# A chunked delta-rule scan in a two-layer decoder: the inverse's products on four quarters of TensorE, and the group norm inside the scan

## The reference, cut to what matters

```python
def step(state, inp):                      # for each of 16 heads of 64
    r_t, d_t, k_t, v_t, kk_t, a_t = inp
    sa = jnp.einsum('bhvk,bhk->bhv', state, -kk_t)
    state = (state * d_t[:, :, None, :] + sa[..., None] * (kk_t * a_t)[:, :, None, :]
             + v_t[..., None] * k_t[:, :, None, :])
    return state, jnp.einsum('bhvk,bhk->bhv', state, r_t)
_, y = lax.scan(step, s0, ...)
mean = jnp.mean(y, axis=-1, keepdims=True)
var = jnp.mean(jnp.square(y - mean), axis=-1, keepdims=True)
y = ((y - mean) * lax.rsqrt(var + GN_EPS)).reshape(B, S, D) * ln_g + ln_b
bonus = jnp.sum(rf * kf * r_k, axis=-1, keepdims=True) * vf
out = (y + bonus.reshape(B, S, D)) * g
return out @ w_o
```

## Time and profile before

| what | us |
|---|---|
| median of three runs | 974.61 (974.09, 974.61, 981.54) |
| profiled execution | 980.12 |
| span of its instructions | 978.3 |
| busy in it: TensorE, weight loads | 856.2, 733.1 |
| busy: VectorE, ScalarE, GpSimd | 660.2, 418.4, 112.1 |
| mean granted clock | 0.945 |

### The profile page before, as it was taken

How to read it: one execution, slowest core, us unless ns; L and a number is a source line. 1 busy time by engine, 2 the same in 40 slices (tenths; PEclk the granted TensorE clock), 3 DMA queues, 4 the chain that set the end, 5 groups by cost and what they waited for, 6 DMA issues and landing times.

```text
span 978.3 us, 17529 instructions
## 1 busy us (share of the span) xinstructions
PE 856.2 (88%) x7477; PEld 733.1 (75%) x7477; DVE 660.2 (67%) x710; ACT 418.4 (43%) x585; POOL 112.1 (11%) x175
## 2 busy tenths in 40 slices
PE   1599997678888888999999999997777899999997
PEld 1597886567776455999999878995445689999976
DVE  4897965557557375999999957365675468545553
ACT  3279222333433146444343355514664653344441
POOL 8400002232331030000000003200000000000000
PEclk9799899799999689999999999996898999999999
DMA  8922335232205307799999556742000538655551
GB/s 322 338 89 85 100 116 197 76 118 88 89 13 189 129 20 258 259 372 368 368 370 384 201 172 208 213 140 77 1 1 1 173 129 278 238 175 194 192 172 43
DMA packets 71837, 170.16 MB, mean 174 GB/s; under 512 B 5432, under 2 KB 6736, under 8 KB 71760
## 3 DMA queue, kind: packets, MB, share of 16 engines
q1 hardware_dynamic: 68784, 160.75, 47.0%
q0 software_dynamic: 2416, 7.15, 2.5%
q10 hardware_dynamic: 560, 1.14, 0.3%
HBM read 166.42 MB, written 1.05 MB: 171 GB/s over the span
## 4 chain that ended last, share of the span: by engine, by line
PE 52%; DVE 34%; ACT 7%; issue 3%; DMA 2%; POOL 1%; ACTq 0%; DVEq 0%; POOLq 0%
DVE wlo L1025 8%; PE ps L1694 5%; PE ps L1698 5%; PE ps L1696 5%; PE ps L1683 5%; PE ps L1686 5%; PE ps L1685 5%; DVE acc L1269 5%; DVE acc L965 3%; PE ps L1620 2%; DVE gt L965 2%; PE ps L1512 2%; PE ps L1514 2%; PE ps L1515 2%; ACT whi L612 2%
## 5 line engine op out<-in xcount | busy, mean ns | idle before, releaser
L1025 DVE TENSOR_TENSOR wlo<-raw,whi 128x2048 fp32r<-128x2048 f32 x94 | 215.5, 2292 | 68.8 <-ACT whi L612 66.8
L612 ACT ACTIVATE whi<-raw 128x2048 fp32r<-128x2048 f32 x94 | 179.2, 1912 | 134.0 <-DMA raw<-in_mlp_down_dram 90.9
L1683 PE MATMUL ps<-ghi,whi 128*128 128x256 f32 x576 | 163.6, 284 | 2.5 <-DVE wlo L1025 1.4
L1686 PE MATMUL ps<-ghi,wlo 128*128 128x256 f32 x576 | 163.0, 283 | 0.0
L1685 PE MATMUL ps<-glo,whi 128*128 128x256 f32 x576 | 163.0, 283 | 0.0
L1683 PEld LDWEIGHTS ps<-ghi,whi 128*128 128x128 f32 x576 | 110.5, 192 | 5.1 <-issue 4.6
L1685 PEld LDWEIGHTS ps<-glo,whi 128*128 128x128 f32 x576 | 110.5, 192 | 0.7 <-issue 0.2
L1686 PEld LDWEIGHTS ps<-ghi,wlo 128*128 128x128 f32 x576 | 110.5, 192 | 0.0
L1694 PE MATMUL ps<-whi,hidhi 128*128 128x512 f32 x256 | 100.9, 394 | 2.4 <-DVE wlo L1025 2.4
L1696 PE MATMUL ps<-whi,hidlo 128*128 128x512 f32 x256 | 99.7, 390 | 0.0
L1698 PE MATMUL ps<-wlo,hidhi 128*128 128x512 f32 x256 | 99.6, 389 | 0.0
(11 more groups left out here) (337 smaller groups left out, 1637.7 us busy)
## 6 DMA issues: line engine op xcount, KB each, us to landing
raw<-in_mlp_up_dram SPq DMA_DIRECT2D x32, 1024.0 KB, 5.7
raw<-in_mlp_down_dram SPq DMA_DIRECT2D x32, 1024.0 KB, 5.2
raw<-in_ada_w_dram SPq DMA_DIRECT2D x24, 1024.0 KB, 6.1
late<-in_ada_w_dram SPq DMA_DIRECT2D x24, 1024.0 KB, 9.6
late<-in_kv_ada_w_dram SPq DMA_DIRECT2D x8, 1024.0 KB, 8.3
raw<-in_kv_w_dram SPq DMA_DIRECT2D x6, 1024.0 KB, 5.3
raw<-in_rw_k_dram SPq DMA_DIRECT2D x4, 1024.0 KB, 9.2
raw<-in_rw_r_dram SPq DMA_DIRECT2D x4, 1024.0 KB, 5.1
```

Source lines behind the costliest of these rows:

```text
L612: sc.activation(whi[i][:, :, :], raw[i][:, :].rearrange("p (k n) -> p k n", k=4), ACT.Copy).then_inc(s_hi, 1)
L1025: st.tell(dv.tensor_tensor(wlo[i][:, :, :], raw[i][:, :].rearrange("p (k n) -> p k n", k=4), whi[i][:, :, :].bitcast(F32), ALU.subtract), ...
L1683: mm(out_, whi[b][:, k, cols], hi[:, k0 + k, :], start=(first and k == 0 and m % 2 == 0), stop=False, skip_group_check=True)
L1686: ins = mm(out_, wlo[b][:, k, cols], hi[:, k0 + k, :], start=False, stop=False, skip_group_check=True)
```

## The change

- **Quarters.** T is kept on the partition half opposite to its transpose. z's matmuls read one half and write the other; p's first kind writes the other half and its second kind the same half, to different banks (2h and 2h+1), and they alternate. start makes T and its transpose by 32 records from t0, which GpSimd now writes ahead of the chunk, during levels 3 and 4 of the chunk before.
- **Order.** The masked copies are an entry of their own (mask), as is ScalarE's copy of krF (copy); each filler has a slot after one of the ten steps of a chunk. An ada piece is split in two entries. Chunk 0's two preps go to banks of their own.
- **Group norm in the scan.** bonus, centre, variance, spread, high and low are entries for one chunk of 64 tokens, one chunk behind or more. The mean is taken out by one matmul with a matrix centre (1 - 1/64 on the diagonal, -1/64 in a head); ln_g is multiplied into gF ahead of the scan (glng), and ln_b and the gate go into the bonus.
- **Out projection.** Its four weight blocks are split in the scan's last chunk and behind it (piece_high, piece_low, by halves), and the first token block is done in eight project entries among the last chunk's norm. The nine keep_clock matmuls ahead of it are gone.
- **ada.** The four pieces of the second layer's part 4 leave the scan's end; one is loaded between the kv and q weights, three between the q and wo weights; their columns are made in the sixth attention unit. acc7's zeroing and its bias loads on GpSimd wait for the last chunk's z.
- **Constants.** s16, tg1, gb1, rs16 and indt have 128 rows instead of 16 or 32, zeroed where unused.

```diff
-ADA_AHEAD = 3
+ADA_AHEAD = 2
+ADA_SLOTS = ((1, 4, 5, 6, 8, 9), (-1, 0, 2, 4, 6, 8), (-1, 0, 2, 4, 6, 8), (-1, -1))
...
-    order = [(x, 0, h) for h in range(2) for x in ("prep", "turn")] + [("values", 0, 0)]
-    ada = ADA_AHEAD
+    ada = [("ada", a, k) for a in range(ADA_AHEAD, ADA_PIECES) for k in range(2)]
+    order = [(x, 0, h) for x in ("prep", "mask", "turn") for h in range(2)]
     for c in range(NCH):
-        until = ADA_PIECES - 2 * (NCH - 1 - c)
-        between = [(x, c - 1, 0) for x in "wusy"] if c else []
+        before, after = c - 1, c + 1
+        slots = [[] for _ in range(10)]
+        order += [("start", c, 0), ("start", c, 1)]
+        if c == 0:
+            slots[0] += [("values", 0, 0)]
+            slots[2] += [("copy", 0, 0), ("bonus", 0, 0)]
+        else:
+            order.append(("u", before, 0))
+            slots[1] += [("s", before, 0)]
+            slots[2] += [("y", before, 0)]
+        if c >= 2:
+            order.append(("high", c - 2, 0))
+            slots[0] += [("cols", c - 2, c + 1)]
+            slots[1] += [("low", c - 2, 0)]
+        order += [ada.pop(0) for n in ADA_SLOTS[c] if n < 0]
         if c + 1 < NCH:
-            between += [(x, c + 1, h) for h in range(2) for x in ("prep", "turn")]
-            between += [("values", c + 1, 0)]
-        order += [("start", c, 0), ("start", c, 1)]
+            slots[0 if c else 6] += [("copy", after, 0)]
+            slots[1] += [("prep", after, 0)]
+            slots[3] += [("mask", after, 0)]
+            slots[4] += [("turn", after, 0)]
+            slots[5] += [("prep", after, 1)]
+            slots[6] += [("w", c, 0)]
+            slots[7] += [("mask", after, 1)]
+            slots[8] += [("turn", after, 1), ("values", after, 0)]
+            if c:
+                slots[5] += [("centre", before, 0)]
+                slots[6] += [("variance", before, 0)]
+                slots[9] += [("spread", before, 0)]
+            slots[9] += [("bonus", after, 0)]
+        else:
+            slots[2] += [("piece_high", 0, 0)]
+            slots[3] += [("piece_high", 0, 1)]
+            slots[4] += [("centre", before, 0), ("piece_high", 1, 0), ("piece_low", 0, 0)]
+            slots[5] += [("piece_low", 0, 1), ("piece_high", 1, 1)]
+            slots[6] += [("w", c, 0), ("variance", before, 0), ("piece_high", 2, 0)]
+            slots[7] += [("spread", before, 0), ("piece_low", 1, 0)]
+            slots[8] += [("piece_high", 2, 1), ("high", before, 0)]
+            slots[9] += [("piece_low", 1, 1), ("low", before, 0)]
+        for n in ADA_SLOTS[c]:
+            if n >= 0:
+                slots[n].append(ada.pop(0))
         for level in range(5):
-            for x in "zp":
+            for i, x in enumerate("zp"):
                 order += [(x, c, 0, level), (x, c, 1, level)]
-                if between:
-                    order.append(between.pop(0))
-                if x == "p":
-                    for _ in range(2):
-                        if ada < until:
-                            order.append(("ada", ada, 0))
-                            ada += 1
-        assert not between
-        while ada < until:
-            order.append(("ada", ada, 0))
-            ada += 1
-        if c in (1, 2):
-            order.append(("cols", c - 1, 2 * min(c + 2, NCH)))
-    return order + [(x, NCH - 1, 0) for x in "wuy"]
+                order += slots[2 * level + i]
+    assert not ada
+    last = NCH - 1
+    return order + [("u", last, 0), ("piece_high", 3, 0), ("piece_low", 2, 0), ("project", 0, 0), ("y", last, 0),
+                    ("piece_high", 3, 1), ("piece_low", 2, 1), ("project", 1, 0), ("centre", last, 0), ("piece_low", 3, 0),
+                    ("project", 2, 0), ("variance", last, 0), ("piece_low", 3, 1), ("project", 3, 0), ("project", 4, 0),
+                    ("spread", last, 0), ("gate", 0, 0), ("high", last, 0), ("low", last, 0),
+                    ("project", 5, 0), ("project", 6, 0), ("project", 7, 0)]
...
-        scan_pieces = (ada_pieces(ada0, 3) + ada_pieces(ada0, 4) + ada_pieces(ada0, 2) + ada_pieces(ada1, 4)
-                       + square(A["rw_o"][0]))
+        scan_pieces = ada_pieces(ada0, 3) + ada_pieces(ada0, 4) + ada_pieces(ada0, 2) + square(A["rw_o"][0])
...
+        place("norm_a", ada_pieces(ada1, 4)[0:1])
         place("q", square(A["nsa_wqg"][0]))
+        place("norm_b", ada_pieces(ada1, 4)[1:4])
...
+            def begun(c, h):
+                js = slice(4 * h, 4 * h + 4)
+                pool.wait_ge(s_xt, 2 * c + h + 1)
+                st.do(level_blocks(c, h, 0))
+                st.tell(g.tensor_tensor(t0[:, js, :], xc[0][:, js, :],
+                                        idc[:, :].unsqueeze(1).to_broadcast([P, 4, N]), ALU.add), ttt[h])
+
             for what, c, h, *level in SCAN:
-                js = slice(4 * h, 4 * h + 4)
-                if what == "start":
-                    pool.wait_ge(s_knr, 2 * c + h + 1)
-                    if c:
-                        pool.wait_ge(s_z_ps[h], 5 * c)
-                    if c >= 2:
-                        pool.wait_ge(s_u_ps, c - 1)
-                    st.do(level_blocks(c, h, 0))
-                    st.tell(g.tensor_tensor(tt[c % 2][:, h, 0, :, :], xc[0][:, js, :],
-                                            idc[:, :].unsqueeze(1).to_broadcast([P, 4, N]), ALU.add), ttt[h])
-                    st.tell(level_blocks(c, h, 1), xct[h])
-                    st.tell(level_blocks(c, h, 2), xct[h])
-                elif what == "z" and level[0] < 3:
+                if what == "start" and c == 0:
+                    begun(0, h)
+                    if h:
+                        for level in (1, 2):
+                            for i in range(2):
+                                st.tell(level_blocks(0, i, level), xct[i])
+                elif what == "z":
                     pool.wait_ge(s_z_ps[h], 5 * c + level[0] + 1)
-                    st.tell(level_blocks(c, h, level[0] + 3), xct[h])
+                    if level[0] < 3:
+                        st.tell(level_blocks(c, h, level[0] + 3), xct[h])
+                    elif c + 1 < NCH:
+                        if level[0] == 3:
+                            begun(c + 1, h)
+                        else:
+                            st.tell(level_blocks(c + 1, h, 1), xct[h])
+                            st.tell(level_blocks(c + 1, h, 2), xct[h])
...
+            for j in range(KC):
+                sc.activation(glng[:, j, :], gF[:, j, :], ACT.Copy, scale=pt1[:, LNG + j:LNG + j + 1])
...
+                if what == "copy":
+                    act.wait_ge(s_kr, c + 1)
+                    if c >= 2:
+                        act.wait_ge(s_y_ps, c - 1)
+                    for e in range(2):
+                        rows = slice(64 * e, 64 * e + 64)
+                        ins = sc.activation(knr[par][rows, :, e, :, :].rearrange("p j a t -> p j (a t)"),
+                                            krF[rows, c, :, :, :].rearrange("p j a t -> p j (a t)"), ACT.Copy)
+                    ins.then_inc(s_krc, 1)
...
-                    sc.activation(tt[par][:, h, 1, :, :].rearrange("p j t -> p (j t)"), bank(h)[:, 0:256], ACT.Copy)\
+                    sc.activation(tt[par][:, h, :, :, :].rearrange("p a j t -> p a (j t)"), ps[:, 2 * h:2 * h + 2, 0:256], ACT.Copy)\
...
+                elif what == "centre":
+                    act.wait_ge(n_mean_ps, c + 1)
+                    sc.activation(sqc[:, :, :].rearrange("p j t -> p (j t)"), bank(7), ACT.Square).then_inc(n_sq, 1)
+                elif what == "variance":
+                    act.wait_ge(n_var_ps, c + 1)
+                    sc.activation(rs16[0:H, :], ps[0:H, 7, 0:N], ACT.Sqrt, scale=1.0 / N, bias=gnepsc[0:H, :]).then_inc(n_gstd, 1)
+                elif what == "high":
+                    act.wait_ge(n_z, c + 1)
+                    sc.activation(zhi[:, :, N * c:N * c + N], yF[:, :, N * c:N * c + N], ACT.Copy).then_inc(n_zhi, 1)
+                elif what == "piece_high":
+                    if c == 0 and h == 0:
+                        act.wait_ge(s_y_ps, NCH - 1)
+                    weight_high(12 + c, h)
...
+                elif what == "mask":
+                    if c == 0:
+                        v.wait_ge(s_zeroed, 1)
...
-                    cur = tt[par][:, h, 0:n, :, :].rearrange("p a j t -> p (a j t)")
-                    st.tell(dv.tensor_tensor(cur, cur, bank(2 + h)[:, 0:256 * n], ALU.add), ttt[h])
+                    cur = tt[par][:, h, 0:n, :, :].rearrange("p a j t -> p a (j t)")
+                    st.tell(dv.tensor_tensor(cur, cur, ps[:, 2 * h:2 * h + n, 256:512], ALU.add), ttt[h])
...
+                elif what == "bonus":
+                    v.wait_ge(n_bb_ps, c + 1)
+                    vc = chunked(vF, c)
+                    st.tell(dv.tensor_tensor(vc, vc, eight(bank(SPREAD(c))), ALU.mult), T["bv"])
```

(48 more changed lines are left out.)

384 lines of the change are left out of this document (191 added, 193 removed).

## The result

The changed kernel takes **950.21 us** (median; 949.58 to 954.78) beside 974.63 for the kernel before on the same chip: ratio 0.974, 95% interval 0.9695 to 0.9786. The forecast was 925 us, in a range of 910 to 942. The sign was right and the gain half of what I had said: 24 us, not 50.

A forecast was written before the change was run, and what follows sets the result against it. Serial engine-after-engine work in prologue and tail, and the scan's chunks, bound the stretch; -13.7 - 0.7 + 2.8 + 3.0 + 0.6 - 41.5 - 1.7 + 1 + 0.6 = -49.6 us took the median 974.61 to 925, range 910 to 942.

The forecast's parts named there:

- Prologue: From the last projection to the scan's first z: earlier preps, copies and zeroing bring first z from 181.7 to 168.0, -13.7 us.
- Tail: From the scan's last add to the out projection's first token block's end: 60.1 falls to 18.6 us, -41.5.
- Later stages: Behind the first token block: second layer norm -1.7 us, attention units +1, late ada pieces +0.6, feed-forward unchanged.
- Prices: Step giving each instruction group's time, such as p group 0.55 us and centre, variance, spread, bonus 0.85 each on TensorE.
- TensorE's own list: TensorE's work in scan and tail: about 26 us in chunks 0 to 2, 20 in chunk 3, 18 in the tail.
- my four chunks: The scan's forecast chunk times: 28.7, 36.2, 37.4 and 28.3 us, changes of -0.7, +2.8, +3.0 and +0.6.
- the walk: Step-by-step timing of engines through prologue, chunks and tail; as it stands it gives 925 us, chance 0.63.
- ScalarE's wait for y: In chunks 1 and 2, ScalarE's krF copy waits for y, delaying state and z copies; VectorE idle 3.6 us in chunk 1.
- Rival (c): Faster groups leave TensorE idle, so stretches of chunks 1 to 3 run at 1.2 GHz: +15 us, 940; chance 0.10.
- Rival (b): Four quarters don't run together in long groups, so p stays 0.96 us: +4, 929; chance 0.12.
- Rival (a): ScalarE's and the norm's waits cost nothing; chunks 1 and 2 take VectorE's list, 28.5 and 29.5 us: 910; chance 0.12.

The follow-up runs named there:

- e5: The changed kernel itself, measured and profiled again: 950.95 us, ratio 0.9706.
- e7: Changed kernel with ScalarE's krF copy in slot 6, unused clock-holding products, and bonus and spread cut to one of eight products: 937.49 us, ratio 0.9561.
- e9: Changed kernel with ScalarE's krF copy in slot 6, and bonus and spread cut to one of eight products: 936.2 us, ratio 0.9599.
- e17: e9 with unused clock-holding products at the turns and ahead of values in chunks 0 to 2: 932.42 us, ratio 0.9513.
- e2: Changed kernel with bonus and spread each issuing one of their eight products: 942.16 us, ratio 0.9645.
- e10: Changed kernel with ScalarE's krF copy in slot 6 and the scan's ada halves over 128 columns instead of 1024: 941.86 us, ratio 0.9654.
- e3: Changed kernel with unused products holding the clock, behind y in chunks 1 and 2, at the turns and ahead of values: 944.37 us, ratio 0.9669.
- e18: e11 with unused clock-holding products at the turns and ahead of values in chunks 0 to 2: 940.35 us, ratio 0.9595.
- e11: Changed kernel with ScalarE's krF copy in slot 6, and bonus and spread (except the last spread) each one wide product: 941.5 us, ratio 0.9638.
- e1: Changed kernel with ScalarE's krF copy for the next chunk in slot 6 instead of slot 0 in chunks 1 and 2: 943.84 us, ratio 0.9654.
- e12: e1 with unused clock-holding products in chunk 0 only: 943.75 us, ratio 0.9661.
- e14: Changed kernel with the padding undone: the two product lists ahead of the scan read 16 and 32 partitions again: 959.05 us, ratio 0.9787.
- e13: Kernel before with only the padding to 128 partitions in the two product lists ahead of the scan: 971.94 us, ratio 0.9923.

## Why the prediction was half right

**Prologue: right.** -13.6 for -13.7, first z 6.0 us behind ScalarE's copy of the last projection.

**Tail: right in its structure,** 20.7 for 18.6. Spread, centre and variance are 1.89, 1.02 and 1.07 us there in e5 where 0.85 each stood, 1.4 of the 2.1. With one product of eight the tail is 1.6 shorter in e7, e9 and e17, and 0.2 in e2, at a granted clock of 0.92.

**Later stages: right,** +0.3 for -0.1, and in their parts: up to the second layer norm's copy -1.3 for -1.7, from there to the hidden copy +0.4 for +0.6, behind it +1.2 for +1. That it is this close is partly luck, as this stretch differs by up to 6 us between profiles.

**The step that failed is "Prices", and with it TensorE's own list,** which I had at "about 26 us in chunks 0 to 2, 20 in chunk 3": 98 of the 130.6 us of my four chunks, so that TensorE would stand for 32.6. It stands for 35.5, near what I had, and is busy for 119.1. e5's scan is 24 us longer than my chunks: 21 are this list, 3 are standing. In all versions without unused products a scan is TensorE's work and 31 to 37 us beside it (38 with the gap of the first profile; 27 in e10, with VectorE's list cut). Of the 21 us:

- *Bonus and spread, 9.* "centre, variance, spread, bonus 0.85 each (estimates, bounded by 0.5 and 1.1 from the same records per column at the full clock)". The seven lists in the scan, four of bonus and three of spread, are 15.0 us (8.2 and 6.8 in e5), 2.1 each. They change weights with every 64 columns. The right row stood in my own group: sixteen records with 128x128 weights over few columns, 2.01 us. I had priced by columns of input, which is nearly right for centre, one product over 512 columns (1.02 to 1.12 at the full clock). Taking seven eighths of these products away shortened the kernel by 8.1, 7.0 and 7.6 in three pairs.
- *Centre and variance, 2.* Put at 0.85 as well, the three centres in e5's scan are 1.12, 1.12 and 2.07 (the last at half the clock), the variances 1.07 each.
- *The granted clock, 4 to 12.* All my prices were at the full clock, and the scan ran at 0.85. Held at 0.94 to 0.96, needed work falls by 9 to 12 (e3: 127.35 with 20 unused products, which are 17 to 20, against 119.08), by 4 to 7 (e17 against e9) and by 8 to 11 (e18 against e11). A turn of four products, 0.5 in the walk, is 1.11 behind a wait in the changed kernel, and 0.60 to 0.66 in four of the six in e3.
- *The rest, 0 to 8,* wasn't taken apart. What the lists above take at half the clock, about 2, counts in two of these terms.

**ScalarE's wait for y: found, placed, and right in sum.** The walk has VectorE idle for 3.6 us in each of two chunks; the copy moved away gives 7.1. It is made up otherwise: in the windows of e5 and e1, 3.6 of TensorE standing and 4.2 of working at a lower clock, the second less certain than the first (e12).

**Rival (c), the clock in the chunks, is the one that came nearest:** 940, at 0.10. Its mechanism was in part what happened (gaps at copy's wait and at the turns), and it should have been a term of the sum, because my own walk contained those gaps, and the earlier trace rows show 0.89 and 0.95 in two chunks without them. But by itself it is 4 to 12, not 15, and the lists' price is as large a part of what was missing.

**Rival (b), quarters: refuted** by 14.6 ns a record. Taking them apart costs 3 to 4 by the times (not outside the intervals), as (b) had it.

**Rival (a), VectorE's own list: refuted** from both sides. No chunk comes near it (28.5 for chunk 1, 37.3 at best), and a list 6 us shorter in each middle chunk brings 2 in all.

**One reading was off:** the 176.19 of the earlier trace rows is where GpSimd's operation starts, not where its result leaves; it lasts 0.72. Nothing in the sum hangs on it.

**What I gave nothing and was worth 5 us** (8 in the times): the 128 rows in the products ahead of the scan. I had counted the memsets that they need and not asked what TensorE does with them. So the miss behind the projections is larger than the total says: 27.0 in the chunks (3.1 of it one gap), 2.0 in the tail, 0.3 in the other stages, less 5.2 ahead. Two errors of opposite sign stood in the sum.

**What stays open:** the rest of the list above; why the padding is worth 3 us more in the times than where it acts; how much slower work the copy's wait costs; and what the gaps of 1 to 3 us without a releaser are.

## What to carry to other kernels

Price a product by what it loads as well as by what it streams: with new weights for every 64 columns, eight products of 128x128 weights are 2 us, however little they compute, and a row of the same form in the trace gives the price. When a walk meets a gap on TensorE, ask at which granted clock the next products run; the waits behind one copy cost 3 us and more of standing, and 7 in all. And when tiles get more partitions "only" with zeros, look at what TensorE did behind the narrow ones: that small edit, alone, gave the kernel before 0.8%, more than a quarter of what the whole change gave.

## What the hardware showed that I had not expected

- 16 records on 16 rows left the following projections at half the clock for 5.3 us (111.2 to 116.5), and for some 3.4 in e14; the same on 128 rows, mostly zeros, left them at the full clock (after, e13).
- Products on 128 and on 32 rows in turn, accumulating, took 10.0 us for 32 records at a granted clock of 1.00; all on 128 rows 7.1.
- 64x64 products in four quarters started every 14.6 ns over 60 records, in fours that start within 20 ns, each record lasting 0.22 us.
- VectorE's reciprocal of 128x512 took 3.35 us, an add of that size 0.69.
